# Identity times identity: matmuls into unfilled PSUM banks during TensorE's long waits in a fused two-block kernel

## The reference, cut to what matters

```python
def first_block(x, ...):
    proj = rms_norm(x, norm1_g) @ w_in
    # q, k: per-head rms_norm and rope; global attention (8 heads) and a
    # dilated windowed attention (8 heads)
    mixed = concatenate([rms_norm(out_a, outa_norm_g), rms_norm(out_b, outb_norm_g)])
    x = x + mixed @ w_out
    return x + conv_ffn(rms_norm(x, norm2_g), w_up, conv_w, conv_b, w_down)

def second_block(x, c, ctx, ...):
    mod_x, mod_c = silu(c) @ w_ada + b_ada, silu(c_ctx) @ w_ada + b_ada
    hx = rms_norm_2(x, norm1) * (1 + sc1) + sh1        # and hc, from ctx, 256 tokens
    # projections, conv over 5 tokens, a chunked state-space scan both ways,
    # windowed attention over latent and context keys
    x = x + g1 * (concatenate([ssd_x, attn_x]) @ w_out)
    h2 = rms_norm_2(x, norm2) * (1 + sc2) + sh2
    x = x + g2 * hier_moe(h2, ...)   # top group of 4, then top 2 of its 8 experts
    return rms_norm_2(x, norm_final)
```

## Time and profile before

| | us |
|---|---|
| median of 3 runs | 1627.4 (1625.85 to 1629.13) |
| profiled execution | 1624.68 |
| its span, first to last instruction | 1622.9 |
| TensorE busy | 1475.3 (91% of the span) |
| TensorE weight loads busy | 1010.2 (62%) |
| VectorE busy | 917.2 (57%) |
| ScalarE busy | 516.2 (32%) |
| mean granted TensorE clock | 0.964 of full speed |
| DMA | 308.35 MB, 190 GB/s on average |

### The profile page before, as it was taken

The page is one execution under the profiler, slowest core; times in us unless marked ns, Lnnn a source line. Parts: engine busy times, 40 slices in busy tenths (PEclk is TensorE's granted clock), DMA queues, the critical chain, the costliest instruction groups (busy, mean ns, idle before and its releaser), DMA issues. The chain is left out here.

```text
span 1622.9 us, 20455 instructions
## 1 busy us (share of the span) xinstructions
PE 1475.3 (91%) x7799; PEld 1010.2 (62%) x7799; DVE 917.2 (57%) x1701; ACT 516.2 (32%) x938; POOL 99.4 (6%) x132
## 2 busy tenths in 40 slices
PE   6899996999999999989998896948999999999896
PEld 5676665788777778877887685724444344344333
DVE  4845774467777667753764677372354344344435
ACT  4445664343353332242426534221111011010102
POOL 0000000000000000001003122001011011000100
PEclk9999997999999999999999999978999999999998
DMA  7222011155444258603010000564999999999994
GB/s 225 78 78 72 1 47 52 52 176 149 137 136 126 92 181 276 209 26 130 26 53 26 2 1 1 207 259 156 409 398 413 402 400 408 398 408 399 409 410 168
DMA packets 112363, 308.35 MB, mean 190 GB/s; under 512 B 13983, under 2 KB 65535, under 8 KB 90763
## 3 DMA queue, kind: packets, MB, share of 16 engines
q1 hardware_dynamic: 102640, 296.33, 49.0%
q0 software_dynamic: 3200, 7.87, 1.5%
q10 hardware_dynamic: 6427, 2.84, 0.7%
HBM read 306.99 MB, written 4.22 MB: 192 GB/s over the span
## 5 line engine op out<-in xcount | busy, mean ns | idle before, releaser
L1299 PE MATMUL bank<-weights_high,hT_high 128*128 128x512 f32 (+2 forms) x736 | 257.7, 389 | 18.3 <-DVE hT_low L1797 5.2
L1299 PE MATMUL bank<-weights_low,hT_high 128*128 128x512 f32 (+2 forms) x560 | 214.5, 383 | 0.0
L1761 DVE TENSOR_TENSOR weights_low<-ring,weights_high 128x2048 fp32r<-128x2048 f32 (+2 forms) x61 | 135.7, 2224 | 136.6 <-ACT weights_high L963 135.7
L963 ACT ACTIVATE weights_high<-ring 128x2048 fp32r<-128x2048 f32 (+2 forms) x61 | 113.5, 1860 | 202.2 <-PE bank L1299 156.8
L1299 PEld LDWEIGHTS bank<-weights_high,hT_high 128*128 128x128 f32 x736 | 140.3, 191 | 46.8 <-issue 11.0
L1299 PE MATMUL bank<-hT_high,weights_high 128*128 128x512 f32 x416 | 164.2, 395 | 1.6 <-DVE hT_low L1799 1.6
L1299 PE MATMUL bank<-hT_low,weights_high 128*128 128x512 f32 x416 | 163.1, 392 | 0.0
L1299 PE MATMUL bank<-hT_high,weights_low 128*128 128x512 f32 x416 | 161.8, 389 | 0.0
L2264 DVE TENSOR_TENSOR hTc<-bank,mod_gain 128x512 f32<-128x512 f32 x32 | 22.1, 691 | 195.7 <-PE bank L1302 195.7
L1299 PE MATMUL bank<-arena,hTc 128*64 128x512 f32 x496 | 116.3, 603 | 8.9 <-DMA arena<-in_w_up 7.3
L1299 PE MATMUL bank<-ring,hTc 128*64 128x512 f32 (+1 forms) x544 | 121.2, 583 | 0.3 <-DMA ring<-in_w_up 0.3
(11 more groups left out here) (324 smaller groups left out, 2353.1 us busy)
## 6 DMA issues: line engine op xcount, KB each, us to landing
arena<-in_w_up SPq DMA_DIRECT2D x32, 1024.0 KB, 20.8
arena<-in_w_down SPq DMA_DIRECT2D x16, 2048.0 KB, 22.5
ring<-in_w_gate SPq DMA_DIRECT2D x32, 1024.0 KB, 18.0
ring<-in_w_up SPq DMA_DIRECT2D x32, 1024.0 KB, 20.0
ring<-in_w_down SPq DMA_DIRECT2D x16, 2048.0 KB, 22.7
arena<-in_w_gate SPq DMA_DIRECT2D x30, 1024.0 KB, 18.9
xn<-in_w_ada SPq DMA_DIRECT2D x48, 512.0 KB, 4.8
ring<-in_w_up SPq DMA_DIRECT2D x44, 512.0 KB, 5.0
```

Source lines behind the costliest of these rows:

```text
L963: high_ready.tick(s.activation(part_view(w_high, key), raw_view(key), ACT.Copy), k)
L1299: return nc.tensor.matmul(o, lhsT, rhs, start=start, stop=stop)
L1761: low_ready.tick(v.tensor_tensor(part_view(w_low, key), raw_view(key), part_view(w_high, key), ALU.subtract), k)
```

## The change

A helper `unread(into, many)` issues `many` f32 matmuls of the identity with itself, 128 columns wide, into the first (or the named) 128 columns of a bank that TensorE has opened and not yet filled. Nothing reads what they write; the transpose or matmul that follows overwrites it. 192 such `mm` are added, in two kinds of places: right after a bank is opened and ahead of a wait, and, in `norm` and for `q2T`, ahead of the last transpose into the last bank. For `xs`, the waits for `u_ready`, `roped_q` and `roped_k` now stand behind the opening of the bank; in `piece` the wait for `y_low_ready` now stands behind that for `piece_added`.

| place | added ahead of the wait | added ahead of the last transpose |
|---|---|---|
| norm1 / mix1 / norm2 / context | 0 / 12 / 4 / 6 | 6 / 5 / 4 / 3 |
| norm1_2 / mix2 / norm2_2 | 4 / 9 / 11 | 12 / 7 / 7 |
| qkT 0 | 9 | |
| probsT, even units of the last three rounds | 5 each | |
| xs 0; q2T 3 | 9 | 6 |
| routing: before "hot"; before "places"; before the first tokens | 16; 34; 6 | |
| first of the last pieces | 7 | |

```diff
--- before.py
+++ after.py
@@ -1301,15 +1301,29 @@
             def tr(o, i, n=P):
                 return nc.tensor.transpose(o, i, ident[0:n, 0:n])
 
+            def unread(into, many):
+
+                for _ in range(many):
+                    mm(into[:, 0:P], ident, ident, True, True)
+
+            UNREAD = {"norm1": (0, 6), "mix1": (12, 5), "norm2": (4, 4), "context": (6, 3), "norm1_2": (4, 12), "mix2": (9, 7),
+                      "norm2_2": (11, 7)}
+
             def norm(name):
 
 
                 _, tiles, parts, _, _ = NORMS[name]
-                opened = [banks.open(pe, ("hT",) + k) for k in halves(name)]
+                opened = []
+                for k in halves(name):
+                    opened.append(banks.open(pe, ("hT",) + k))
+                    if k[1] == 0:
+                        unread(opened[0], UNREAD[name][0])
                 for i, t in enumerate(tiles):
                     normed.wait(pe, (name, t, parts[-1][0]))
                     for k in halves(name):
                         j = k[1]
+                        if t == tiles[-1] and j == KT - 1:
+                            unread(opened[j][:, i * P:(i + 1) * P], UNREAD[name][1])
                         last = tr(opened[j][:, i * P:(i + 1) * P],
                                   xn[:, t, :].rearrange("p (q j) -> p j q", j=KT)[:, j, :])
                         if t == tiles[-1]:
@@ -1328,6 +1342,8 @@
             def heads_transposed(n):
                 if 0 <= n < 16:
                     bank = banks.open(pe, ("qkT", n))
+                    if n == 0:
+                        unread(bank, 9)
                     qk_ready.wait(pe, n)
                     for j in range(4):
                         last = tr(bank[:, j * P:(j + 1) * P], pj[:, n % 3, j * P:(j + 1) * P])
@@ -1377,6 +1393,8 @@
                 if 1 <= q <= NP:
                     for n in (2 * q - 2, 2 * q - 1):
                         bank = banks.open(pe, ("probsT", n))
+                        if q >= NP - 2 and n % 2 == 0:
+                            unread(bank, 5)
                         prob.wait(pe, n)
                         for k in range(TT):
                             last = tr(bank[:, k * P:(k + 1) * P], probs[:, n % 4, k * P:(k + 1) * P])
@@ -1508,11 +1526,13 @@
                                                      hT_high[:, j, :], hT_low[:, j, :])):
                         last = mm(bank[:, :], a, b, j == n == 0, j == KT - 1 and n == 2)
                 banks.close(last, ("xbc", m, c))
-            u_ready.wait(pe, KT - 1)
-            roped_q.wait(pe, TT - 1)
-            roped_k.wait(pe, TT - 1)
             for t in range(AT):
                 bank = banks.open(pe, ("xs", t))
+                if t == 0:
+                    unread(bank, 9)
+                    u_ready.wait(pe, KT - 1)
+                    roped_q.wait(pe, TT - 1)
+                    roped_k.wait(pe, TT - 1)
                 for m in range(4):
                     last = tr(bank[:, m * P:(m + 1) * P], u[:, m, t * P:(t + 1) * P])
                 banks.close(last, ("xs", t))
@@ -1536,6 +1556,8 @@
                 bank = banks.open(pe, ("q2T", j))
                 roped_q.wait(pe, TT - 1)
                 for t in range(TT):
+                    if j == t == 3:
+                        unread(bank[:, t * P:(t + 1) * P], 6)
                     last = tr(bank[:, t * P:(t + 1) * P], q2[:, t, j * P:(j + 1) * P])
                 banks.close(last, ("q2T", j))
             tok_copied.wait(pe, ("b", AT - 2))
@@ -1639,10 +1661,12 @@
             for t in range(TT):
                 last = mm(ps[1][:, t * 36:(t + 1) * 36], lgT[:, t * P:(t + 1) * P], C("both_halves"), True, True)
             route_pe.tick(last, "logits")
+            unread(ps[2], 16)
             route.wait(pe, "hot")
             hot = osum.rearrange("p t e -> p (t e)")
             mm(ps[2][:, 0:TT * E], C("before"), hot, True, True)
             route_pe.tick(mm(ps[2][:, TT * E:2 * TT * E], C("one").broadcast_to([P, P]), hot, True, True), "rank")
+            unread(ps[3], 34)
             route.wait(pe, "places")
             for n in range(8):
                 last = mm(ps[3][:, 0:2 * NBLK], hot_p[:, n, :], hot_b[:, n, :, :].rearrange("p a b -> p (a b)"), n == 0,
@@ -1704,9 +1728,11 @@
 
 
 
-                pe.wait_ge(y_low_ready, results)
                 if added is not None:
                     pe.wait_ge(piece_added, added)
+                if n == LAST_PIECES[0][0] * TT:
+                    unread(ps[4], 7)
+                pe.wait_ge(y_low_ready, results)
                 for k, place in enumerate(places):
                     for part, y in enumerate((y_high, y_low)):
                         for half in range(2):
@@ -1720,6 +1746,7 @@
                 n = pair * TT + t
                 piece(n, t, [2 * pair % 4, 2 * pair % 4 + 1], 2 * pair + 2, n - 1 if n >= 2 else None)
 
+            unread(ps[0], 6)
             tokens_in_place(0, 0, 0)
             route_act.wait(pe, "rows")
             for n in range(E):
```

## The result

| | before | after |
|---|---|---|
| median of 8 runs each, same chip, us | 1626.62 (1623.59 to 1633.53) | 1616.31 (1615.05 to 1625.43) |
| ratio, 95% interval | | 0.9933 (0.9912 to 0.9954) |
| profiled execution / its span, us | 1624.68 / 1622.9 | 1615.08 / 1613.2 |
| mean granted clock | 0.964 | 0.980 |
| TensorE busy, us | 1475.3 | 1504.9 |

The account below looks back on a forecast made before the run. Bound: up to 1117 us TensorE's chain with DVE/ACT, its clock low behind waits; from 1130 DMA through the experts. Seven terms summed to 10.3 us saved; from the 1627.4 median that gave 1617.0 us, range 1610.5 to 1625.0.

Parts of the forecast that it names:

- The price and the cover: An identity product costs 0.22 us at the high clock level, 0.43 low; at the high level all groups are covered.
- Rival 2: Slower: products run at the low level in the routing and overrun waits; about 9.6 us lost, 1637; chance 0.07.
- Rival 1: The clock level falls all the same after what is left of the waits; saving 4.8 us, 1622.5; chance 0.13.
- mix1, norm2_2, halves, last pieces: Saved at full clock: mix1's transposes 2.1 us, norm2_2's transposes 1.7, the halves 1.6, the last pieces 1.0.
- norm1 and qkT 0: norm1's products save 0.6 us in the projection (0 to 2.3); those at qkT 0 save 0 (0 to 1.4).
- norm1_2: Its low stretch of 22 records would run at full clock: 1.5 us saved, bounds 0 to 2.5.
- Routing: Rank products save 0.4 us and the table 1.6; of these 2.0, 1.4 was taken.
- Expert 0: Its low first records save at most 2.2 us; taken as 0.4, a DMA wait and DVE's scaling still ahead.
- Carry to the end: What is won ahead of the first expert-slot reload at 1117.27 us moves all reloads and reaches the end one for one.
- Rival 4: It does not carry: wins ahead of the experts only lengthen the wait for weights or tokens; 1626.4 us; chance 0.07.
- xs, q2T, mix2: Products there save 0: what TensorE waits for next is DVE or ACT work independent of the transposes' pace.
- third rival: Transposes count as idle for the clock: no gain at halves, norm1_2 and half of mix1; 1621 us; chance 0.03.

Follow-up runs that it names:

- e4: Changed kernel with every count of products doubled (places 68, hot 32 and so on): 1631.52 us, 1.0009 of before.
- e8: The changed kernel itself, executed again unaltered: 1619.53 us, 0.9937 of before.
- e7: Changed kernel with more products in the waits left (norm1_2 4 and 20, places 43, others) and two new places: 1615.63 us, 0.9912 of before.
- e11: Changed kernel with nearly every wait over 1.3 us ahead of the experts filled, also in the weave (scan and windowed attention): 1610.18 us, 0.9896 of before.
- e2: Changed kernel without products at norm2, context, mix2, qkT, probsT, xs and q2T: 1620.89 us, 0.9948 of before.
- e5: Kernel before plus products only at norm2_2, "hot", "places" and the first tokens: 1625.76 us, 0.9969 of before.
- e6: Kernel before plus only 6 products ahead of the first tokens and 7 ahead of the last pieces: 1627.67 us, 0.9988 of before.
- e9: Changed kernel without the products at xs, q2T and mix2: 1620.81 us, 0.9957 of before.
- e10: Kernel before plus products only at xs, q2T, mix2 and 12 ahead of a 3.33-us wait in the weave: 1626.60 us, 0.9996 of before.
- e1: Changed kernel with every identity product replaced by two transposes of the identity: 1620.44 us, 0.9946 of before.
- e12: e11 without its products in the weave of scan and windowed attention: 1618.51 us, 0.9935 of before.
- e3: Changed kernel with only the products at norm2, context, mix2, qkT, last attention rounds, xs and q2T: 1625.51 us, 0.9984 of before.

## Why the prediction was right, point by point

The mechanism held. How much of each term is the change and how much one execution, the other profiles tell. The table leaves out e4, whose doubled counts overrun the waits; the counts in brackets are profiles:

| stretch, us | without products there | with them |
|---|---|---|
| start to the first score (norm1's products) | 138.38 to 141.11 (5) | 139.73 to 143.33 (8) |
| mix1 to the next product | 6.94 to 8.17 (5) | 5.55 to 5.64 (8) |
| norm1_2 to the cumulative sum | 21.20 to 22.05 (5) | with 4 and 12: 21.10 to 21.14 (4), 19.60 (1); with 4 and 20: 19.60 (3) |
| norm2_2 to the halves | 8.03 to 9.03 (4) | 6.46 to 6.50 (9) |
| halves to ranks | 12.48 to 12.67 (4) | 10.97 to 10.99 (9) |
| ranks to table | 11.37 to 11.38 (4) | 10.86 to 10.87 (9) |
| table to first tokens | 9.43 to 9.53 (4) | with 34: 7.80 to 9.60 (6); with 43: 7.72 to 7.88 (3) |
| expert 0 to the first reload | 9.40 to 9.50 (3) | with 6: 7.12 to 10.05 (7); with 9 to 16: 7.12 to 9.21 (3) |
| last pieces | 5.98 to 6.22 (3), 4.97 (1) | 4.97 to 4.98 (9) |

So mix1, norm2_2, the halves, the ranks and the last pieces take their short time in every profile that has the products (the last pieces once without them too), some 7 us in all against the profile of before. The table and expert 0 are won in some executions, and the start is no gain at all.

- **The price and the cover.** Right: 0.23 us a product at 1.00 against 0.22. At mix1 the 12 products began low and took 4.48 us, inside the bounds of 2.6 and 5.2, and 0.32 us of the wait were left. Rival 2's routing did not come in the changed kernel; e4 shows the overrun that it describes.
- **Rival 1** came true in part: at the three waits that it names (norm1, norm1_2, places) a low stretch followed what was left of the wait.
- **mix1, norm2_2, halves, last pieces**: 2.33, 1.55, 1.53 and 1.03 against 2.1, 1.7, 1.6 and 1.0. The mechanism showed as named: ACT's first drain at mix1 starts 1.40 us after the start of DVE's last tile (267.48), where the earlier trace rows had 3.7. The products with `w_out` are released by DVE's `hT_low`, which in turn waited 1.39 us for that drain:

```profile
268.88 5.46 ACT L1023 ACTIVATE hT_high<-bank,const,gains 128x512 fp32r<-128x512 f32 x8 [1.63 <-PE bank L1302]
```

- **norm1 and qkT 0** (0.6 and 0): wrong by 2 us in this pair, and in kind. A loss was outside both bounds. The products ahead of the last transpose hold back bank 7, and on ACT's queue the issues of the small input loads stand behind the wait for that bank. The first of them, in the timeline of ACT's queue of after:

```profile
15.26 0.34 ACTq L1029 DMA_DIRECT2D const<-tables  x1
```

  and in e4, with 12 products:

```profile
17.21 0.34 ACTq L1029 DMA_DIRECT2D const<-tables  x1
```

  In both, as in before (14.73), that is 0.04 to 0.05 us behind the end of the norm's last transpose. DVE waits for a later one of these loads before it touches the first heads (timeline of DVE, after):

```profile
35.24 0.42 DVE L1843 TENSOR_SCALAR arena<-arena 128x64 f32<-128x64 f32 x2 [12.11 <-DMA route_w<-in_w_expert]
```

  This row starts at 34.74 to 35.56 in the five profiles without products at norm1 and at 35.24 to 37.81 in the nine with them, and the first heads follow 9.1 to 9.2 us later in all fourteen. So what is won in the projection ends at a DMA, and the products there are no gain and in most profiles go with a loss of one or two us for the first heads. That they cause it is read from these rows alone: no run changes only them. I had named DVE's and ACT's drains as what waits for that bank, and not the DMA issues behind ACT's. In the pair itself 0.35 us were won up to the heads and 1.78 lost from there to the first score. The new low stretch at 76.7 accounts for that: 3.4 us of full work, half of them lost. It stands behind the 1.82-us wait that before has too, without one. I had no term for a low stretch at a place with no cover.
- **norm1_2** (1.5): 0.8. 2.52 us of wait were left and a low stretch followed, now 3.4 us long instead of nearly 7. e8, with the same 12, had none there and gained 2.3; so did e7 and e11, with 20.
- **Routing** (1.4): 0.6. The ranks' 0.5 came; the table's 1.6 did not in this profile, since a low stretch of 6.8 us began with it, behind the 2.56 us left idle. With 34 products the way from the table to the tokens took 9.4 to 9.6 us in three profiles, 8.4 in two and 7.80 in e2; with 43 and 0.55 left it was 7.7 to 7.9 in all three. I had discounted 2.0 by 0.6 for this, which left the table 1.0; over the six profiles it gained nothing three times, 1.1 twice and 1.7 once.
- **Expert 0** (0.4): 2.3, the largest miss. I took the six products as too few, with a DMA wait and DVE's scaling still ahead. They were enough in three of seven profiles; e8, the same program, gained 0.6 here. This was luck, and so was the 1.1 us between the first reload and the last pieces, for which I had no term. The two, 3.0 us above the forecast, made up for the 3.5 missed at norm1, norm1_2 and in the routing: the sum is closer than its terms.
- **Carry to the end.** Right: the first reload 7.6 us earlier (I had about 9), the last pieces 8.7, the end 9.7. Rival 4 is refuted.
- **xs, q2T, mix2** (0 each): right in this pair, open over many executions. The profiles of e5 and e6 show low stretches between xs and the weave (853 to 872 us) and in it that the one profile of before had not; e9's shows no loss there, and the ratios of e9 and e10 do not tell a gain from none. The gain by the median (10.9 us by the ratio) is larger than the 9.7 of the pair, but the interval of 3.4 us to either side does not settle it.

**The transposes.** The third rival is refuted: e1 settles what the earlier trace rows suggested: a filler of transposes alone, in front of transposes alone, keeps 1.00. The rule in the Trainium skill (TensorE: Matmul & The Clock Gate, Part 4: PE-mode transpose), that the clock does not engage for transposes, does not hold in this kernel (0.9946 by e1, where the rule would leave about 1.00).

## What to carry to other kernels

Where TensorE's clock falls behind its waits, as it does here, fill each wait with unread work of known price until some half a microsecond is left, not until it is halved: the same program gained 0.67% with waits of 1.5 to 2.6 us left and 1.04% with nearly all filled, some of them at places that the first change did not touch. Count the price against the wait first, since doubling the counts lost everything. One profile shows one draw of where the level falls. Before you credit a place with what one pair of profiles shows, look at the same stretch in others: expert 0 gave 2.3 us in one profile of the changed kernel and 0.6 in the next.

## What the runs showed of the hardware that was not expected

- Which waits a low stretch follows is not told by their length alone, and no run here shows what decides it: in the changed kernel 2.62 us at 41.7 was followed by none, 1.60 at 927.7 and 1.44 at 978.7 by one each, 1.82 at 73.6 by one, while in before the same 1.81 us had none.
- In the experts, where TensorE is busy for some 66 of 70 us, there are 20 to 31 us of low stretches between the first reload and the last pieces in each of the 14 profiles, whatever was filled ahead. DMA was 0.99 busy from 1130 to 1200 us in before, and their cause was not looked for.
- The same program differs by 10 to 15 us between executions (before 1622.4 to 1639.1 over all comparisons), and with more waits filled the spread is narrower: the changed kernel's runs lie within 10.4 and 8.6 us, e11's six within 3.9, e7's six within 2.2. That the low stretches make the whole spread is not shown; in e5's and e6's profiles they stand where 5.8 and 6.9 us were lost.
- The distance from the first reload to the last pieces is not constant: 488.6 to 492.0 us in the profiles of after, e11, before, e12, e9 and e6. The forecast had it fixed.
- Left open: a kernel like e11 without products at norm1 was not run; by the point on norm1 it should be up to a microsecond or two faster at the first heads, if the wait behind them hides none of it. Nor was the changed kernel run without its qkT or attention groups alone, so their worth is known only as part of e2 and e3.
